# Routing from the raw residual rows, gathers without padded rows, and a later wait for the stored rows, in a one-core diffusion layer

## The chip, the cores and the metric

The kernel runs on one core of a Trainium2 chip. The metric is the device time of one execution in microseconds (us). Before the change it is 688.88 us, the median of three runs (688.39 to 688.99).

## The reference

All arrays are fp32. One layer works on 512 latent tokens and 256 context tokens of width 1024. The first half (modulated RMS norm, input projection, neighbourhood attention beside a gated linear recurrence, output projection) gives the residual rows x. What the change touches comes after it:

```python
hx = _rms(x, norm_ffn[l]) * (1 + sc_fx) + sh_fx
x = x + g_fx * _moe(hx, router_w, router_b, exp_w1[l], exp_w3[l], exp_w2[l])

def _moe(h, router_w, router_b, w1, w3, w2):
    aff = jax.nn.sigmoid(h @ router_w)            # 512 x 16
    sel = aff + router_b
    # best of 4 groups by the sum of its two best, then the two best experts in it
    wts = ...                                     # their affinities, normalised
    for e in range(16):
        y = (jax.nn.silu(h @ w1[e]) * (h @ w3[e])) @ w2[e]
        out = out + gates[..., e:e + 1] * y
```

`sc_fx` and `sh_fx` are pieces of `silu(c) @ w_mod + b_mod`. An expert has 6 MB of weights, all sixteen 96 MB, which are read once.

## The kernel before

It is written engine by engine: each has its own program, and semaphores tie them. The order of the work is the order in which those programs are written; there is no scheduler.

**Modulation sums.** DVE multiplies pieces of `w_mod` by the condition vector and adds them up over rows into `acct`; PE (`reduce_mod`, L1398 to L1407, called four times between the projections) sums over partitions by eight matmuls against a column of ones, and DVE (`reduced`, L893) adds the bias. The result is `ab2`: per column a scale (index 0) and a shift (index 1), as [128, 8]. DVE completes it at L996 and L997.

**Attention and out projection.** PE runs 17 rounds: scores, transposed probabilities, values, and a share of the out projection (`project_out`, L1540) in each. Two of the 64 out projection products are left for after the rounds. DVE turns the out projection into residual rows `x2` (`residual`, L1036), four tiles j of 128 tokens in two halves each.

**Router.** ACT squares and roots the rows (`square2`, `root2`), DVE takes the reciprocal and makes `xn = x2 * 1/rms` (`normalise`, L1048). PE transposes `xn` in eight blocks (`router`, L1573), ACT and DVE each evacuate four blocks, one by one, and apply scale and shift on the way (`router_rows`, L706 and L1052). PE multiplies by the router weights `rw` (`logits`, L1587), ACT takes the sigmoid (L723). DVE then selects experts in some 60 small operations, PE counts and sorts (L1616 to L1625), and DVE writes `slot_tok`: for each tile of 32 slots the row numbers of its tokens (L1234). A slot without a token points to one of 512 spare rows behind the real ones.

**Rows through DRAM.** Each row is stored as four quarters of 256. POOL stores `xn` into `xn_quarters`, and one tile again into the spare rows (L472), then `x2` into `out_quarters` (L476, L478). It then waits for all these stores and for the slots, and gathers the first four tiles (L486), 128 quarter rows each. Later gathers follow one per tile, and each tile's result is added to `out_quarters` by an accumulating scatter (L490).

**Experts.** For each tile DVE transposes the gathered rows and applies scale and shift (L1251, L1253, L1260). PE multiplies by w1 and w3 (`products`, L1640), then by w2 (`rows_out`, L1655). Every expert has at least two tiles.

**Weights.** SP fetches 48 chunks of 2 MB (`fetch`, L309), three per expert: two halves of w1 and w3, then w2. There are 11 places for them. Chunks 0 to 10 wait for whatever lies in their place before; the others wait for PE to be done with the chunk 11 before them:

```python
sp.wait_ge(y_ps, 2 * NT)
for n in range(5, 8):
    fetch(n)
sp.wait_ge(xn_out, 8 * NT + 16)
sp.wait_ge(xn_out1, 8 * NT)
sp.wait_ge(h2_ps, 2 * NT)
fetch(8)
sp.wait_ge(acc_in, 16 * NT + 16)
fetch(9)
sp.wait_ge(slots_turned, 1)
fetch(10)
```

## Time and profile before

| | |
|---|---|
| median of three runs | 688.88 us (688.39 to 688.99) |
| the profiled execution's own time | 685.32 us |
| its span, first to last instruction | 683.6 us |
| busy in the span | PE 605.4 us, PE weight loads 362.8, DVE 385.0, ACT 199.0, POOL 180.0 |
| moved by DMA | 168.08 MB, mean 246 GB/s |
| mean granted clock of TensorE | 0.949 of 2.4 GHz |
| attention rounds | about 264 to 371 us |
| router and selection, first gather landed | 371 to 417 us |
| experts | 419 to 670 us, last stores to the end |

PE is TensorE's matmul side. Busy time of matmuls is modelled, and neighbouring groups overlap a little, so a group's end is best read from the start of the next. A span's times are counted from its first instruction; the execution's own time is 1.72 us longer than its span.

### The profile page before, as it was taken

To read this page: it belongs to the slowest core of one execution; us is meant where nothing else is said; L and a number is where in the kernel's file an instruction comes from. 1 tells how busy PE (TensorE), PEld (TensorE's weight loads), DVE (VectorE), ACT (ScalarE), POOL (GpSimd) and SP (SyncE) were. 2 spreads that over 40 slices of the span, in tenths; PEclk is the share of its full clock that TensorE was granted. 3 is DMA by queue.
4 is the path that set the end of the run, shared out by engine and by line. 5 is a ranking of instruction groups with operands and counts; after the bars stand their busy time and mean duration, and the time that the engine had idled before them with its cause. 6 is when DMAs were issued, how large, how long until landed. Compare 5 with 4: busy or idle time off the path is not lost.

```text
span 683.6 us, 14771 instructions
## 1 busy us (share of the span) xinstructions
PE 605.4 (89%) x5803; PEld 362.8 (53%) x5803; DVE 385.0 (56%) x909; ACT 199.0 (29%) x499; POOL 180.0 (26%) x202
## 2 busy tenths in 40 slices
PE   0799999999999998999999824999999999879981
PEld 0455544455554444555556822667767776635650
DVE  4714995686869874786775472444444444414430
ACT  5312201158796203555465400001000110000000
POOL 4044782000000001000000203454445554424421
PEclk9999999999999999999999557999999999989996
DMA  8989338530305175900007986699999999999974
GB/s 300 387 277 310 124 123 291 201 124 0 123 1 185 53 255 160 253 4 1 1 0 296 424 339 279 240 389 390 390 393 390 387 389 390 387 409 391 394 247 138
DMA packets 52979, 168.08 MB, mean 246 GB/s; under 512 B 4212, under 2 KB 26384, under 8 KB 42688
## 3 DMA queue, kind: packets, MB, share of 16 engines
q1 hardware_dynamic: 41136, 145.78, 55.6%
q0 software_dynamic: 11664, 21.53, 12.2%
q8 instruction: 37, 0.61, 0.3%
q14 instruction: 14, 0.11, 0.0%
q10 hardware_dynamic: 128, 0.04, 0.0%
HBM read 155.53 MB, written 13.12 MB: 247 GB/s over the span
## 4 chain that ended last, share of the span: by engine, by line
PE 69%; DVE 10%; DMA 8%; ACT 4%; issue 4%; SPq 3%; ACTq 0%; POOLq 0%; DVEq 0%
PE bank L1640 18%; PE bank L1446 12%; PE bank L1655 9%; PE bank L1556 7%; DMA ring<-in_exp_w_dram 6%; PE bank L1371 6%; PE bank L1378 4%; SPq L313 3%; PE bank L1533 2%; PE bank L1508 2%; PE bank L1519 2%; DVE acct L868 1%; PE bank L1404 1%; DMA pre<-xn_quarters,slot_tok 1%; ACT hx L553 1%
## 5 line engine op out<-in xcount | busy, mean ns | idle before, releaser
L1446 PE MATMUL bank<-ring,hx 128*128 128x512 f32 x256 | 117.8, 617 | 2.5 <-DVE mix L923 1.9
L1640 PE MATMUL bank<-pre 128*32 128x256 f32 x1248 | 77.1, 392 | 17.7 <-DVE pre L1260 9.6
L1446 PEld LDWEIGHTS bank<-ring,hx 128*128 128x128 f32 x256 | 49.7, 197 | 62.7 <-issue 60.3
L729 ACT ACTIVATE pre<-bank 128x128 f32<-128x128 f32 x44 | 12.2, 277 | 223.8 <-PE bank L1640 198.2
L1260 DVE TENSOR_TENSOR pre<-pre,ab 128x256 f32<-128x256 f32 x44 | 19.2, 437 | 94.6 <-PE bank L1640 83.7
L1640 PE MATMUL bank<-ring,pre 128*32 128x256 f32 x1152 | 68.1, 380 | 3.0 <-issue 1.7
L1640 PEld LDWEIGHTS bank<-pre 128*32 128x32 f32 x1248 | 46.6, 113 | 42.7 <-DVE pre L1260 11.2
L1556 PE MATMUL bank<-ring,mix 128*128 128x512 f32 x128 | 60.7, 594 | 0.0
L1640 PEld LDWEIGHTS bank<-ring,pre 128*32 128x32 f32 x1152 | 43.6, 110 | 23.5 <-issue 4.8
L490 POOL DMA_INDIRECT out_quarters<-pre,cur_s x22 | 35.4, 1610 | 71.2 <-DVE pre L1278 52.8
L490 POOL DMA_INDIRECT out_quarters<-hx,cur_s x22 | 35.7, 1624 | 51.5 <-DVE hx L1278 49.2
L1655 PE MATMUL bank<-pre 128*32 128x256 f32 x704 | 42.6, 379 | 0.9 <-DVE pre L1271 0.9
L1271 DVE STREAM_TRANSPOSE pre<-pre 128x128 f32<-128x128 f32 x44 | 18.2, 415 | 44.6 <-PE bank L1655 44.6
L1371 PE MATMUL bank<-hx,ring 128*128 128x256 f32 (+1 forms) x128 | 42.0, 488 | 1.4 <-DVE hx L846 1.4
L460 POOL DMA_DIRECT2D pre<-pre x1 | 0.6, 561 | 157.0 <-ACT pre L665 157.0
L486 POOL DMA_INDIRECT hx<-xn_quarters,cur_g x30 | 31.1, 1035 | 14.2 <-issue 8.8
L1371 PEld LDWEIGHTS bank<-hx,ring 128*128 128x128 f32 x128 | 24.1, 190 | 19.1 <-issue 16.7
L1655 PE MATMUL bank<-ring,pre 128*32 128x256 f32 x544 | 34.1, 390 | 0.0
L1655 PEld LDWEIGHTS bank<-pre 128*32 128x32 f32 x704 | 27.1, 110 | 12.0 <-DVE pre L1271 1.4
L470 POOL DMA_DIRECT2D xn_quarters<-pre x4 | 2.2, 544 | 110.6 <-DVE pre L1049 110.6
L868 DVE SCALAR_TENSOR_TENSOR acct<-ring,cs,acct 128x256 f32<-128x256 f32 x56 | 29.4, 525 | 2.0
L1556 PEld LDWEIGHTS bank<-ring,mix 128*128 128x128 f32 x128 | 21.7, 190 | 14.7 <-issue 14.7
(282 smaller groups left out, 1013.2 us busy)
## 6 DMA issues: line engine op xcount, KB each, us to landing
pre<-in_exp_w_dram SPq DMA_DIRECT2D x28, 1024.0 KB
ring<-in_exp_w_dram SPq DMA_DIRECT2D x24, 1024.0 KB
ring<-in_w_mod_dram SPq DMA_DIRECT2D x16, 1024.0 KB, 5.1
pre<-in_exp_w_dram SPq DMA_DIRECT2D x8, 2048.0 KB
ring<-in_exp_w_dram SPq DMA_DIRECT2D x6, 2048.0 KB
ring<-in_w_in_dram SPq DMA_DIRECT2D x5, 2048.0 KB, 14.1
ring<-in_w_mod_dram SPq DMA_DIRECT2D x4, 2048.0 KB, 18.1
mix<-in_exp_w_dram SPq DMA_DIRECT2D x6, 1024.0 KB
```

Source lines behind the costliest of these rows:

```text
L313: sp.dma_start(chunk13(e, part)[:, :, w, :], src[0, ORDER[e]].rearrange("(p k) n -> p k n", p=P)[:, 4 * part:4 * part + 4, :]).then_inc(cs ...
L486: g.indirect_dma_start(out=xg[par], out_offset=None, in_=xn_dram, in_offset=bass.IndirectOffsetOnAxis(ap=index.bitcast(U32), axis=0)).then ...
L490: g.indirect_dma_start(out=acc_dram, out_offset=bass.IndirectOffsetOnAxis(ap=cur_s[par][:].bitcast(U32), axis=0), in_=ysb[par], in_offset= ...
L868: ins = v.scalar_tensor_tensor(out=dst, in0=src[:, k, :], scalar=cs[:, k, 0:1], in1=dst, op0=ALU.mult, op1=ALU.add)
L1260: v.tensor_tensor(blocks(hsT), blocks(xm), wide(1), ALU.add).then_inc(hs_ready, 1)
L1271: v.transpose(eT.rearrange("p (b t) -> p b t", b=4), eact.rearrange("p (t b) -> p b t", b=4)).then_inc(t2_ev, 1)
L1371: ins = te.matmul(B[bank][:, 0:n], slot[:, k, P * m:P * (m + 1)], hxT[:, k, lo:lo + n], start=(k == 0), stop=(k == KD - 1))
L1378: ins = te.matmul(B[4 + m % 2][:, :], slot[:, k, P * m:P * (m + 1)], hxT[:, k, 0:T], start=(k == 0), stop=(k == KD - 1))
L1446: ins = te.matmul(B[bank][:, :], hxT[:, k, P * j:P * (j + 1)], slot[:, k, :], start=(k == 0), stop=(k == KD - 1))
L1556: ins = te.matmul(B[YB[hf]][:, :], mix[:, k, P * j:P * (j + 1)], out_at[hf][0][:, k, :], start=(k == MW), stop=(k == MW - 1))
L1640: ins = te.matmul(H_[R * q:R * (q + 1), 0:2 * P].rearrange("p (w n) -> p w n", w=2), hsT[:, R * k:R * (k + 1)], w[:, k % 4, :, P * q:P * ( ...
L1655: ins = te.matmul(Y_[R * q:R * (q + 1), 0:QD], eT[:, R * c:R * (c + 1)], w[:, c, QD * q:QD * (q + 1)], start=(c == 0), stop=(c == 3))
```

## The change

The shared parts of it:

- The router transposes `x2` instead of `xn`, half a tile (four blocks) at a time, so that a token's 1/rms is applied to its 16 logits instead of its 1024 values (`logit_rows`). The scale goes into the weights (`rws = rw * scale`), the shift into one row of 16 numbers (`shift_sum`, summed over partitions by one more matmul, L1624 of the new kernel). Evacuation is a plain copy of 512 columns. The logits come from PSUM banks 5 and 6.
- The sets of transposes for tile 0 stand inside the last rounds, those for tile 1 ahead of the last two out projection products.
- ACT normalises tiles 2 and 3, behind the sigmoid; DVE keeps 0 and 1.
- Columns are spread over partitions in two halves of 4 x 128 instead of 8 x 128. So the modulation sums take four matmuls per call, `xn` is stored with its columns reordered, and a half of w1 or w3 is one contiguous megabyte.
- The gathers get a bound: a row number beyond the real rows is left out. The spare rows of `xn_quarters` and the store into them go.
- SP issues chunk 8 ahead of its wait for the transposes. POOL waits for the stored `x2` after the first four gathers.

```diff
-    xn_dram = nc.dram_tensor("xn_quarters", (TRASH + 4 * P, QD), F32, kind="Internal").ap()
+    xn_dram = nc.dram_tensor("xn_quarters", (TRASH, QD), F32, kind="Internal").ap()
@@ SP
-                                     src[0, ORDER[e]].rearrange("(p k) n -> p k n", p=P)[
-                                         :, 4 * part:4 * part + 4, :]).then_inc(csem[n % NH], 16)
+                                     src[0, ORDER[e], 512 * part:512 * (part + 1), :].rearrange(
+                                         "(p k) n -> p k n", p=P)).then_inc(csem[n % NH], 16)
-            sp.wait_ge(xn_out, 8 * NT + 16)
+            sp.wait_ge(xn_out, 8 * NT)
             sp.wait_ge(xn_out1, 8 * NT)
+            fetch(8)
             sp.wait_ge(h2_ps, 2 * NT)
-            fetch(8)
@@ POOL
-            g.dma_start(xn_dram[TRASH:TRASH + 4 * P, :].rearrange("(p q) n -> p (q n)", q=CB), xn[:, 0, :]).then_inc(
-                xn_out, 16)
...
-                    ap=index.bitcast(U32), axis=0)).then_inc(xg_in[par], 16)
+                    ap=index.bitcast(U32), axis=0), bounds_check=TRASH - 1, oob_is_err=False).then_inc(xg_in[par], 16)
...
-            pool.wait_ge(acc_in, 16 * NT + 16)
             pool.wait_ge(slots_turned, 1)
             for n in range(4):
                 gather(slot_tok[:, n:n + 1], n)
             pool.wait_ge(plan_in, 1)
+            pool.wait_ge(acc_in, 16 * NT + 16)
@@ ACT
-                for k in range(MW):
-                    a.activation(h2T[:, j % 2, k, :], B[RB[j % 2]][:, P * k:P * (k + 1)],
-                                 ACT.Identity, scale=ab2[:, 0, k:k + 1], bias=ab2[:, 1, k:k + 1]).then_inc(h2_ev, 1)
+                a.activation(h2T[:, j % 2, 4 * h:4 * h + 4, :].rearrange("p k t -> p (k t)"), B[XB[j][h]][:, :],
+                             ACT.Copy).then_inc(done, 1)
...
-            act.wait_ge(lg_ps, NT)
-            a.activation(rt[:, 0:NT * NE], B[0][:, 0:NT * NE], ACT.Sigmoid).then_inc(aff_ready, 1)
+            act.wait_ge(logit_in, NT + 1)
+            a.activation(rt[:, 0:NT * NE], rt[:, 256:256 + NT * NE], ACT.Sigmoid).then_inc(aff_ready, 1)
+            for j in (2, 3):
+                act.wait_ge(roots_set, j)
+                a.activation(xn[:, j, :].rearrange("p (q h m) -> p h q m", q=CB, h=2),
+                             x2[:, j, :].rearrange("p (h q m) -> p h q m", q=CB, h=2), ACT.Copy,
+                             scale=small[:, 24 + j:25 + j]).then_inc(xn2_ready, 1)
@@ DVE
+            link(v.tensor_tensor(rws, rw[:], ab2[:, 1, :].unsqueeze(2).to_broadcast([P, KD, NE]), ALU.mult))
+            link(v.tensor_reduce(shift_sum, rws.rearrange("p k e -> p e k"), AX.X, ALU.add))
+            v.tensor_tensor(rws, rw[:], ab2[:, 0, :].unsqueeze(2).to_broadcast([P, KD, NE]), ALU.mult).then_inc(
+                rws_ready, 1)
...
+            def logit_rows(j):
+                v.scalar_tensor_tensor(out=rt[:, 256 + NE * j:256 + NE * (j + 1)], in0=B[LB[j]][:, NE * j:NE * (j + 1)],
+                                       scalar=small[:, 24 + j:25 + j], in1=a1[:].rearrange("p k s -> p (k s)"),
+                                       op0=ALU.mult, op1=ALU.add).then_inc(logit_in, 1)
@@ PE
-                for k in range(KD):
-                    ins = te.matmul(B[7][HD * (n % 2):HD * (n % 2 + 1), k:k + 1],
-                                    acct[:, :].rearrange("p (m k) -> p m k", k=KD)[:, :, k], ones[:, 0:1], start=True,
-                                    stop=True)
+                for k in range(4):
+                    ins = te.matmul(B[7][:, k:k + 1], acct[:, :].rearrange("p (m k) -> p m k", k=4)[:, :, k], ones[:, 0:1],
+                                    start=True, stop=True)
...
+            def router(j, h):
+                if j == 1 and h == 0:
+                    pe.wait_ge(prob_done, NA)
+                if j >= 2:
+                    pe.wait_ge(h2_ev if h == 0 else h2_ev2, j - 1)
+                pe.wait_ge(x2_ready, 2 * j + h + 1)
+                for k in range(4):
+                    ins = te.transpose(B[XB[j][h]][:, P * k:P * (k + 1)],
+                                       x2[:, j, :].rearrange("p (h m k) -> p h m k", h=2, k=4)[:, h, :, k], ident[:])
+                ins.then_inc(h2_ps, 1)
```

PE's program at the end of the attention rounds, before. L1519 transposes probabilities, L1533 multiplies by the values, L1556 is the out projection, L1582 the router's transposes, L1593 the logits:

```order
L1533 MATMUL bank<-pre 64x128
L1582 MATMUL bank<-ident,pre 128x128 [waits xn2_ready]
L1582 MATMUL bank<-ident,pre 128x128 x7
L1556 MATMUL bank<-ring,mix 128x512 [waits ot_ev]
L1556 MATMUL bank<-ring,mix 128x512
L1582 MATMUL bank<-ident,pre 128x128 [waits xn2_ready,ot_ev,pt_ev]
L1582 MATMUL bank<-ident,pre 128x128 x7
L1593 MATMUL bank<-rw,pre 128x16 [waits h2_ev,rw_in]
```

The same place in the new kernel, where L1581 is the out projection, L1593 the transposes and L1616 the logits:

```order
L1558 MATMUL bank<-pre 64x128
L1593 MATMUL bank<-ident,hx 128x128 [waits x2_ready,prob_done]
L1593 MATMUL bank<-ident,hx 128x128 x3
L1593 MATMUL bank<-ident,hx 128x128 [waits x2_ready]
L1593 MATMUL bank<-ident,hx 128x128 x3
L1581 MATMUL bank<-ring,mix 128x512 [waits ot_ev]
L1581 MATMUL bank<-ring,mix 128x512
L1624 MATMUL bank<-pre,ones 128x16
L1616 MATMUL bank<-pre 128x16 [waits h2_ev] x4
```

Tile 0's transposes have moved up, to before the last transposed probabilities, and tile 1's stand where tile 0's stood; they wait for residual rows and not for normalised ones. The matmul of the shift comes in.

DVE's program from the last residual rows to the first operation of the selection, before (L1044 and L1045 residual, L1064 reciprocal, L1049 normalise, L1058 evacuation, L1110 to L1116 constants, L1128 selection):

```order
L1045 TENSOR_TENSOR hx<-hx,pre 128x512 [waits dch]
L1064 RECIPROCAL small<-small 128x1 [waits rt2]
L1049 TENSOR_SCALAR pre<-hx,small 128x1024 [waits dch]
L1058 TENSOR_SCALAR pre<-bank,ab 128x128 [waits h2_ps]
...
L1058 TENSOR_SCALAR pre<-bank,ab 128x128 [waits lg_ps,h2_ps]
L1058 TENSOR_SCALAR pre<-bank,ab 128x128 x3
L1110 MEMSET pre 128x4 x16
L1113 MEMSET pre 128x4 [waits dch]
L1113 MEMSET pre 128x4 x3
L1116 MEMSET counts 128x16 [waits dch]
L1128 TENSOR_TENSOR pre<-pre,rb 128x64 [waits rw_in,aff_ready,dch]
```

And in the new kernel (L1063 residual, L1076 evacuation, L1080 reciprocal, L1085 scaled logits, L1137 to L1143 constants, L1154 selection):

```order
L1063 TENSOR_TENSOR hx<-hx,pre 128x512 [waits dch]
L1076 COPY pre<-bank 128x512 [waits lg_ps,h2_ps]
L1080 RECIPROCAL small<-small 128x1 [waits rt2]
...
L1080 RECIPROCAL small<-small 128x1 [waits rt2]
L1085 SCALAR_TENSOR_TENSOR pre<-bank,small,a 128x16 [waits lg_ps,roots_set]
L1137 MEMSET pre 128x4 x16
L1140 MEMSET pre 128x4 [waits dch]
L1140 MEMSET pre 128x4 x3
L1143 MEMSET counts 128x16 [waits dch]
L1154 TENSOR_TENSOR pre<-pre,rb 128x64 [waits aff_ready,dch]
```

The normalise operations are gone from this stretch, and the constants stand behind an operation that waits for the last logits (`lg_ps`), where before they stood behind an evacuation.

## Rows read from the trace of the kernel before

**Rows 1.** Its DMA view, 434 to 657 us, by queue: packets, MB, share of 16 engines

```profile
q1 hardware_dynamic: 8699, 76.45, 83.2%
q0 software_dynamic: 7550, 10.29, 20.3%
```

**Rows 2.** Timeline of PE: start, us, what, count, [idle before and its releaser]

```profile
604.13 3.64 PE L1640 MATMUL bank<-pre 128*32 128x256 f32 x32 [4.05 <-DMA pre<-in_exp_w_dram]
...
657.01 1.93 PE L1640 MATMUL bank<-ring,pre 128*32 128x256 f32 x32 [1.37 <-DMA ring<-in_exp_w_dram]
```

**Rows 3.** Timelines of PE and, last row, DVE, 373 to 391 us

```profile
373.99 1.05 PE L1582 MATMUL bank<-ident,pre 128*128 128x128 f32 x8
374.87 1.86 PE L1593 MATMUL bank<-rw,pre 128*128 128x16 f32 x16
377.62 1.68 PE L1582 MATMUL bank<-ident,pre 128*128 128x128 f32 x8 [0.90 <-DVE pre L1049]
379.10 3.44 PE L1593 MATMUL bank<-rw,pre 128*128 128x16 f32 x16
382.37 1.95 PE L1582 MATMUL bank<-ident,pre 128*128 128x128 f32 x8
384.11 6.85 PE L1593 MATMUL bank<-rw,pre 128*128 128x16 f32 x32
...
372.47 1.37 DVE L1058 TENSOR_SCALAR pre<-bank,ab 128x128 f32<-128x128 f32 x4 [0.78 <-PE bank L1582]
```

**Rows 4.** Windows: PE, PEld, DVE, ACT, POOL busy, granted clock, DMA share, GB/s

```profile
376.00:378.00 2.00, 1.10 (x10) 1.04 (x10) 1.97 (x5) 1.45 (x4) 0.23 (x1) 1.00 1.09 463
378.00:380.00 2.00, 2.00 (x12) 2.00 (x11) 1.96 (x7) 1.63 (x5) 0.40 (x2) 0.50 0.94 401
658.00:660.00 2.00, 2.00 (x44) 1.20 (x40) 0.62 (x2) 0.37 (x2) 0.00 (x0) 1.00 0.74 239
```

**Rows 5.** Timeline of DVE, constants and start of the selection

```profile
385.67 0.29 DVE L1110 MEMSET pre<- 128x4 f32 x16
...
391.31 0.23 DVE L1128 TENSOR_TENSOR pre<-pre,rb 128x64 f32<-128x64 f32 x1 [5.04 <-issue]
```

**Rows 6.** Chain of waits (start, us, what), and SP's timeline, fetch 9

```profile
410.86 6.29 DMA pre<-xn_quarters,slot_tok
...
408.10 0.80 SPq L313 DMA_DIRECT2D hx<-in_exp_w_dram  x2
```

**Rows 7.** Chain of waits, 240 to 262 us

```profile
245.97 2.01 PE bank L1404 x16
```

**Rows 8.** Timelines of ACT and DVE, third gate after the third modulation sum

```profile
175.50 0.69 ACT L616 ACTIVATE pre<-bank,half_b 128x512 f32<-128x512 f32 x1
...
174.18 1.28 DVE L953 TENSOR_TENSOR_SCAN pre<-pre 128x512 f32<-128x512 f32 x1
```

**Rows 9.** Timeline of DVE, the first score

```profile
265.55 0.42 DVE L1010 TENSOR_TENSOR hx<-bank,pre 128x256 f32<-128x256 f32 x1 [7.57 <-PE bank L1508]
```

**Rows 10.** Tile xn_quarters, stores issued by POOL

```profile
DMA to landing us min/median/max: 9.0/10.6/13.7
```

**Rows 11.** DMA view, 424 to 433 us: busy tenths in 40 bins, and POOL's queue

```profile
DMA  0000000000096500000300000000000000000000
...
q0 software_dynamic: 48, 0.13, 5.3%
```

**Rows 12.** The page's groups: the shift of a tile, once per tile

```profile
L1260 DVE TENSOR_TENSOR pre<-pre,ab 128x256 f32<-128x256 f32 x44 | 19.2, 437 | 94.6 <-PE bank L1640 83.7
```

**Rows 13.** DMA view, 664 to 674 us: POOL's queue, scatters alone

```profile
q0 software_dynamic: 432, 0.39, 34.9%
```

**Rows 14.** Timeline of POOL, one scatter and one gather in the stream

```profile
582.06 1.58 POOL L490 DMA_INDIRECT out_quarters<-pre,cur_s  x1 [2.76 <-DVE pre L1278]
583.95 1.10 POOL L486 DMA_INDIRECT hx<-xn_quarters,cur_g  x1 [0.30 <-issue]
```

More of the change, by code:

```diff
@@ L194, in build @@
          cur_g_ready, cur_s_ready, acc_in, gf_ps, gf_ev, lane_set, sil_warm, pad_ready, bank_z,
[L195 removed]
+         row_sum_ready, scale_ready, hc_ready, h2_ev2, rows_taken, xm_scaled, act_ready, ffn_in,
+         half_ps, rws_ready, logit_in, roots_set) = [sem(n) for n in names]
         xg_in = [sem(f"rows_in{par}") for par in range(4)]
@@ L1048, in normalise @@
             def normalise(j):
-                v.tensor_scalar(xn[:, j, :], x2[:, j, :], small[:, 24 + j:25 + j], None,
+                v.tensor_scalar(xn[:, j, :].rearrange("p (q h m) -> p h q m", q=CB, h=2),
+                                x2[:, j, :].rearrange("p (h q m) -> p h q m", q=CB, h=2), small[:, 24 + j:25 + j], None,
                                 ALU.mult).then_inc(xn2_ready, 1)
@@ L1082, in _ @@
             router_rows(0)
+            router_rows(1)
             residual(2 * NT - 2)
             residual(2 * NT - 1)
+            router_rows(3)
             roots_in(2, 2, 3)
-            normalise(2)
-            router_rows(1)
+            dve.wait_ge(lg_ps, NT - 1)
+            v.tensor_copy(a1[:].rearrange("p k s -> p (k s)"), B[5][:, NT * NE:(NT + 1) * NE]).then_inc(logit_in, 1)
+            dve.wait_ge(logit_in, 1)
+            for j in range(NT - 1):
+                logit_rows(j)
             roots_in(3, 3, 4)
-            normalise(3)
-            router_rows(2)
-            router_rows(3)
+            dve.wait_ge(lg_ps, NT)
+            logit_rows(NT - 1)
             NTE = NT * NE
```

87 lines of the change are left out of this document (42 added, 45 removed).

## Prediction

> **What bounds the kernel now.** The page shows PE busy nearly everywhere, so I read it stage by stage. Four stages matter here.
>
> The expert stage, from 434 us on, is bound by the transfer of the expert weights. In 434 to 657 the two data queues together fill the 16 DMA engines (83.2% and 20.3%) [rows 1]. PE consumes weights faster than they come: it stood 4.05 us waiting for them before 604.13, and 1.37 us before its last weight chunk at 657.01 [rows 2]. So the end follows the time at which this stream starts, and the traffic it shares the DMA engines with. The stream starts when PE has finished its third tile (about 432 us): until then every buffer is full.
>
> Before it lies a serial stretch, 371 to 419 us: out projection, transposes (L1582), logits (L1593), sigmoid, selection on DVE, one matrix that sorts tokens into slots, and the first gather. PE sets the pace up to the sigmoid: 16 logit matmul records took 1.74 to 1.86 us at 374.87 and 3.3 to 3.4 us from 379.10 on [rows 3], because the granted clock was 1.00 (2.4 GHz) until 378 us and 0.50 (1.2 GHz) after it [rows 4]. DVE starts its selection 0.35 us after the last logit matmul, its constants having been written at 385.67 [rows 5]. The first gather then took 6.29 us to land, on the chain [rows 6].
>
> Further ahead, the modulation sums (L1404) take 2.01 us of PE each, and the fourth stands on the chain at 245.97 [rows 7]. After its end PE goes straight on with projections to 262.3 us.
>
> **The change, part by part.**
>
> *Modulation sums.* Each of four calls now issues 4 matmuls instead of 8, over 128 columns of weights instead of 64. Before, 16 records took 2.01 us, 0.126 us each; 128-column weight loads with a tiny moving side cost about the same (1.86 us for 16 at full clock [rows 3, 7]). So each call saves 1.0 us. Only the fourth counts: after the third, ACT waited for PE but its next step (L616 at 175.50) also waited for the DVE scan that began at 174.18 and took 1.28 us [rows 8], so that stage is paced by ACT and DVE, not PE; bounds for the first three are 0 and 0.1. The three added DVE operations (L1012 to L1014 of the new kernel, under 1.2 us together) come when DVE is idle for 7.6 us before the first score [rows 9], and would cost 1.2 us without that idle time. Everything behind 246 us moves **1.0 us** earlier (bounds 0 and 1.1).
>
> *Transposes and logits.* The transposes read x2, so none waits for a normalise; the 0.90 us that PE stood before the third set [rows 3] goes. In exchange the first two sets (1.05 us each) stand ahead of the last two out projection products, where one stood before, so the last residual rows are ready about 0.6 us later (1.05 us, less what DVE gains by copying 512 columns once instead of four pieces in 1.37 us [rows 3]). They are not late: the last half set of transposes needs them some 8 us further on. Added on PE: one matmul for the shift, 0.23 us. On PE's own times I get, from 371.1 us: values end 372.1, second set 373.2, out projection 374.9, shift 375.1, logits(0) 376.9, third set 377.9. If the clock falls at 378 us as it did, three logit groups at 3.3 to 3.4 and two half sets at 0.87 (3.27 + 1.74 + 6.78 = 11.8 us) end at 389.8, against 390.96: 1.15 us saved. Then comes what is new behind the last logit matmul: DVE scales the last rows (0.2 us, as its small operations take, and 0.1 us of handover) and writes its constants only after that, 0.6 us that formerly were hidden [rows 5]. So selection starts 0.95 us after PE instead of 0.35. Net **0.6 us** saved. Bounds: 0.6 us lost, if the 1.15 doesn't come; 6.3 us gained, if the clock stays at 1.00 through the logits (12.96 us from 378 on at half clock become about 6.1 from 377.9).
>
> *Residual and normalised rows.* Rows 2 and 3 are normalised by ACT behind the sigmoid, about 390.3 to 392.7 us (512 columns took it 0.69 us [rows 8], so some 1.2 us each), so their stores are issued at 392 to 393 instead of 377.8 to 379.9; those behind them on POOL's queue, five stores of x2, go too, at 393 to 396. The stores took 9.0 to 13.7 us to land on a full DMA [rows 10]; 393 + 13.7 = 407 is still before the slots are ready at 409. So nothing waits for them. One store of 0.5 MB is gone, and there is a hole of 2 us in the DMA's work. On SP, the ninth weight chunk (fetch 8) waits for these stores and comes at 395 to 397 instead of 394.19; fetch 9 waits for all x2 stores and I put it at 405.5 to 408 against 408.10 [rows 6]; fetch 10 follows the slots. They are first used by the third and fourth experts, tens of us later, so their own lateness is free. POOL's wait for the x2 stores is behind the first gathers; before it had ended (408.1) ahead of the slots (410.0), so moving it gives 0 now.
>
> *The first gather.* It waited behind weights: 6.29 us loaded; alone on the DMA, one issued at 424.91 moved its data in bins 11 to 14 of 40 over 424 to 433, that is by 427.2, 2.3 us after issue [rows 11]. With fetch 9 ahead by 0 to 2.6 us, less of it is in the queue. Bounds: 0 and 4.0 us saved; I take **0.8**, nearer 0, because fetch 10 is still issued just ahead of it, and tile 0 has no padded row. The Trainium skill, "DMA: Bandwidth & Descriptors", Queues, rings and completion order, says that each engine alternates between its queues packet by packet; by that the gather's few packets would never sit behind a backlog and this term would be 0. The 6.29 against 2.3 us speaks against it.
>
> *The gathers in the stream.* 44 tiles of 128 quarter rows [rows 12] make 5632, of which 4096 are real (512 tokens, 2 experts, 4 quarters), so 27% of the gathered rows fall away. One gather alone took 5.3% of 9 us on all 16 engines, 0.48 us [rows 11]; a scatter, 34.9% of 10 us for 0.39 MB, three of them, 1.16 us [rows 13]. In the stream the pair cost 20.3% of 223 us over 39.5, 1.15 us [rows 1], of which the gather's share is 0.34 us (0.48/1.64). Saved: 39 x 0.27 x 0.34 = 3.6 us at most if spread evenly (5.1 at 0.48), 0 if a left out row costs what a moved one does. But a weight chunk has landed only when its slowest part has, and the parts end unevenly: the DMA share falls to 0.74 at 658 to 660 and takes some 5 us to run out [rows 4]. The padded rows are always the last of a tile's 32. From the routing of the reference (expert counts 122, 102, 129, 57, 67, 90, 87, 88, 19, 17, 17, 17, 51, 67, 59, 35) rows 0 to 3 are empty in 12.5% of the 44 tiles and rows 28 to 31 in 45%. If the part that gates serves the first rows, 39 x 0.125 x 0.34 = 1.7 us is saved. I take **2.5 us**, about midway between 1.7 and 3.6.
>
> The weight transfers for w1 and w3 read whole megabytes instead of every second 8 KB; pieces keep 8 KB, and the engines are full with both, so 0 (bounds: 2 us either way). xn's changed column order alters patterns, not counts.
>
> **Sum:** 1.0 + 0.6 + 0.8 + 2.5 = 4.9 us. The profiled execution took 685.32 us (span 683.6), so 680.4; the median of the runs is 3.56 us above it, at 688.88, so I forecast 684.0.
>
> **The rivals.**
>
> *A, the stream saves what its slowest part saves, or nothing.* For: the uneven ends. 1.0 + 0.6 + 0 to 0.8 + 0 to 1.7 gives 684.8 to 687.3; I take 686.3. The Trainium skill, "DMA: Bandwidth & Descriptors", The descriptor swizzle, ties each DMA engine to fixed partitions, four neighbours at a time; by that the engines of rows 0 to 3 would save only the 1.7 us. No row here shows single engines.
>
> *B, the clock stays up longer in the logits.* PE has no pause of 0.90 us and its dense out projection ends 0.9 us later. One later step is worth about 1.7 us, all of it 5.7. 682.3, down to 678.3. Against: the mix of work is the same, and from 382 to 391 it never brought the clock back.
>
> *C, PE waits longer at the end and drops its clock.* Near 600 us, after a wait of 4.05, 32 records took 3.64 us instead of 1.93 [rows 2], and lost 1.7 us beside the wait. If the earlier wait shrinks, PE is ready for its last chunk some 3 us sooner and waits there; 13 us of tiles follow, of which a part at half clock costs 2 to 3.5 us: 686.8.
>
> *D, slower: the check makes POOL's gathers slow.* POOL spends per tile 1.10 us on the gather, 1.58 on the scatter and 0.30 before each [rows 14], 3.3 of the 5.4 us per tile (418.8 to 657.0, 44 tiles). Up to 2.0 us more per gather is hidden but for the first, which is on the path. At 3.3 us per gather it would cost 2.2 us there and 0.2 x 40 = 8 later: 694. From an added 2.2 us it outweighs the gains. Nothing in the trace speaks for it; an index compared with a constant is little work.
>
> *E, the rows are not left out, or the front gains nothing*: about 688.
>
> **How the numbers follow.** Forecast mechanism 0.42, A 0.20, B 0.17, C 0.10, D 0.05, E 0.06. What a measurement can tell from no change is about 0.2%, 1.4 us: 687.5 to 690.3 is "same". Faster: all of the forecast and B (0.59), most of A (0.15) and over half of C (0.06): 0.80. Same: the rest of A, C and E, 0.13. Slower: D and a little of the unknown weight order, 0.07. The range takes in A, C and B's first step: 680.5 to 688.0.
>
> **What would show it.** Four modulation calls of 8 records in 1.0 us. L1616 groups without a pause before the third transposes; last logit matmul about 2 us earlier than 390.96 (1.0 from the sums, 1.15 here), with the constants written after it. Gather landing in 5 to 6 us. In the stream, the gathers' queue with fewer bytes (about 8.9 MB instead of 10.3) and the last weight wait at about 652. The forecast is wrong if the queue's bytes don't fall, if the weight queue's rate changes, or if the granted clock around 380 us or after 650 us is another.

## The result, and the profile after

The changed kernel takes 683.09 us (median of four executions, 682.84 to 684.1) beside 688.93 us for the kernel before (688.39 to 689.43): a ratio of 0.9918, 95% interval 0.9901 to 0.9935. The forecast was 684.0. The profiled execution took 682.84 us, its span 681.0, so the two profiled executions differ by only 2.5 us where the medians differ by 5.8: the one of before was 3.6 under its median, the one of after is a typical one. That is why the table below has each kernel twice, the second time from a later session (their spans: 686.4 and 678.0). All numbers are differences of start times in the timelines, in us; "the logits' end" is the start of the matmuls that stand behind them on PE (L1637, L1610 before).

| stretch | before | again | after | again |
|---|---|---|---|---|
| start to first score on DVE | 265.55 | 266.42 | 263.26 | 264.94 |
| to the logits' end | 125.34 | 125.31 | 122.52 | 121.75 |
| to the selection's start | 0.42 | 0.42 | 1.08 | 1.08 |
| to the slots written | 18.41 | 18.46 | 18.72 | 18.73 |
| to the gather's issue | 1.14 | 1.14 | 1.22 | 1.21 |
| gather, issue to landing | 6.29 | 6.33 | 7.02 | 4.60 |
| to the stream's first fetch | 15.06 | 15.05 | 14.82 | 15.18 |
| to PE's last wait for weights, its end | 224.80 | 225.32 | 223.11 | 222.90 |
| to the end of the span | 26.59 | 27.95 | 29.25 | 27.61 |

So against the second profile of before, the more typical one, the change gains 1.5 to 3.2 us before the first score, 2.8 to 3.6 in the router (0.66 of it paid back for the constants), and 2.2 to 2.4 in the stream. The gather varies by itself, and 0.3 us is lost between the selection's start and the slots. The end is longer in one profile of before and in both of after.

The gain before the first score is mostly not the change's own. In fourteen profiles, with those of the experiments below, the granted clock fell to half in one to three short stretches between 28 us and the first score. They add up to 10.2, 10.2 and 13.6 us in the three profiles whose program is still that of before up to this point (first score at 265.6, 266.4 and 268.6), and to 3.4 us in six, 6.8 in two and 10.2 in three of the eleven of the changed one. In these last three the first score came at 266.2 to 267.0, no earlier than in before with the same 10.2 us. Whether the change itself makes these stretches fewer is not shown.

The fourth modulation sum on the chain of waits of the changed kernel ([rows 7] before: 16 records, 2.01 us):

```profile
245.86 1.64 PE bank L1430 x8
```

A record with 128 columns of weights costs 0.205 us on average, one with 64 columns 0.126: half as many records do not take half the time.

PE through the router ([rows 3] before), start, us, what, count:

```profile
370.00 1.23 PE L1593 MATMUL bank<-ident,hx 128*128 128x128 f32 x8
371.07 1.88 PE L1581 MATMUL bank<-ring,mix 128*128 128x512 f32 x4
372.79 0.29 PE L1624 MATMUL bank<-pre,ones 128*128 128x16 f32 x2
372.93 1.94 PE L1616 MATMUL bank<-pre 128*128 128x16 f32 x16
374.71 1.19 PE L1593 MATMUL bank<-ident,hx 128*128 128x128 f32 x8
375.74 1.86 PE L1616 MATMUL bank<-pre 128*128 128x16 f32 x16
377.44 1.02 PE L1593 MATMUL bank<-ident,hx 128*128 128x128 f32 x4
378.26 3.43 PE L1616 MATMUL bank<-pre 128*128 128x16 f32 x16
381.53 1.09 PE L1593 MATMUL bank<-ident,hx 128*128 128x128 f32 x4
382.42 3.43 PE L1616 MATMUL bank<-pre 128*128 128x16 f32 x16
385.78 1.08 PE L1637 MATMUL bank<-gfx,ones 128*32 128x256 f32 x8
```

No group has an idle time in front of it, and the third transposes start behind the first logits at once. The clock, [rows 4] before:

```profile
376.00:378.00 2.00, 2.00 (x18) 2.00 (x18) 0.00 (x0) 0.59 (x2) 0.00 (x0) 0.90 1.02 401
378.00:380.00 2.00, 2.00 (x12) 2.00 (x11) 0.00 (x0) 1.50 (x3) 0.00 (x0) 0.50 0.98 414
```

It fell at about the same time, but the program is some 2 us further on, so two logit groups, not one, ran in 1.9 us. The same time on the axis is a coincidence of these two profiles: counted from the start of the last out projection products, the clock fell after 5.7, 5.8 and 7.0 us in the three profiles of before's program and after 6.5 to 10.9 us in the eleven of the changed one. DVE then writes its constants behind the last scaled row ([rows 5] before: 5.6 us ahead of the selection). DVE's timeline, from the second profile of the changed kernel (a_again):

```profile
387.06 0.37 DVE L1137 MEMSET pre<- 128x4 f32 x16
387.50 0.10 DVE L1140 MEMSET pre<- 128x4 f32 x4
387.66 0.07 DVE L1143 MEMSET counts<- 128x16 f32 x1
387.77 0.23 DVE L1154 TENSOR_TENSOR pre<-pre,rb 128x64 f32<-128x64 f32 x1
```

The selection starts behind the last of them. The gather of the first profile on the chain, and SP's fetches 9 and 10 beside it ([rows 6] before):

```profile
406.80 7.02 DMA pre<-xn_quarters,slot_tok
```

```profile
406.69 0.80 SPq L317 DMA_DIRECT2D hx<-in_exp_w_dram  x2
407.55 1.24 SPq L317 DMA_DIRECT2D pre<-in_exp_w_dram  x2
```

The stream, 434 to 650 us ([rows 1] before), and PE's waits in it ([rows 2] before):

```profile
q1 hardware_dynamic: 8604, 74.95, 84.2%
q0 software_dynamic: 7648, 8.88, 19.6%
```

```profile
597.24 1.93 PE L1667 MATMUL bank<-pre 128*32 128x256 f32 x32 [2.30 <-DMA pre<-in_exp_w_dram]
...
645.93 1.93 PE L1667 MATMUL bank<-ring,pre 128*32 128x256 f32 x32 [2.51 <-DMA ring<-in_exp_w_dram]
651.75 3.64 PE L1667 MATMUL bank<-ring,pre 128*32 128x256 f32 x32 [3.89 <-DMA ring<-in_exp_w_dram]
```

The wait of 4 us that stood near 604 has become one of 3.89 before the last chunk, and what follows it runs at half clock at first: 32 records in 3.64 us instead of 1.93.

### The profile page after: what moved, and what is told of

It reads as the page before. It is cut to its first block, busy times and chain, and to the rows that moved or that the text cites. A ratio compares the mean times of both kernels' runs of the same rounds, so it can differ in the third digit from the quotient of the medians.

```text
span 681.0 us, 14746 instructions
## 1 busy us (share of the span) xinstructions
PE 598.6 (88%) x5773; PEld 358.3 (53%) x5773; DVE 382.8 (56%) x902; ACT 197.9 (29%) x490; POOL 185.5 (27%) x201
## 4 chain that ended last, share of the span: by engine, by line
PE 63%; DMA 13%; DVE 11%; ACT 5%; issue 4%; SPq 1%; ACTq 0%; POOLq 0%; DVEq 0%
PE bank L1667 16%; PE bank L1471 9%; PE bank L1682 8%; PE bank L1581 7%; DMA ring<-in_exp_w_dram 6%; PE bank L1397 6%; DMA pre<-in_exp_w_dram 5%; PE bank L1404 4%; PE bank L1558 2%; PE bank L1533 2%; PE bank L1544 2%; DVE acct L882 1%; PE bank L1616 1%; DMA pre<-xn_quarters,slot_tok 1%; SPq L317 1%
## 5 line engine op out<-in xcount | busy, mean ns | idle before, releaser
L1471 PE MATMUL bank<-ring,hx 128*128 128x512 f32 x256 | 114.4, 602 | 5.6 <-DVE mix L936 4.9
L1667 PEld LDWEIGHTS bank<-pre 128*32 128x32 f32 x1248 | 46.1, 111 | 39.7 <-DVE pre L1286 12.2
L1581 PE MATMUL bank<-ring,mix 128*128 128x512 f32 x128 | 60.7, 594 | 0.0
L490 POOL DMA_INDIRECT hx<-xn_quarters,cur_g x30 | 34.4, 1148 | 14.2 <-issue 8.9
L476 POOL DMA_DIRECT2D xn_quarters<-pre x4 | 2.2, 542 | 121.8 <-DVE pre L1067 97.2
L1682 PEld LDWEIGHTS bank<-pre 128*32 128x32 f32 x704 | 27.0, 113 | 13.6 <-issue 1.6
L1397 PEld LDWEIGHTS bank<-hx,ring 128*128 128x128 f32 x128 | 24.1, 190 | 19.1 <-issue 16.7
L1581 PEld LDWEIGHTS bank<-ring,mix 128*128 128x128 f32 x128 | 21.7, 190 | 14.7 <-issue 14.7
## 6 DMA issues: line engine op xcount, KB each, us to landing
pre<-in_exp_w_dram SPq DMA_DIRECT2D x8, 2048.0 KB, 26.6
```

What stands on the lines that cost most here:

```text
L490: g.indirect_dma_start(out=xg[par], out_offset=None, in_=xn_dram, in_offset=bass.IndirectOffsetOnAxis(ap=index.bitcast(U32), axis=0), boun ...
L1397: ins = te.matmul(B[bank][:, 0:n], slot[:, k, P * m:P * (m + 1)], hxT[:, k, lo:lo + n], start=(k == 0), stop=(k == KD - 1))
L1471: ins = te.matmul(B[bank][:, :], hxT[:, k, P * j:P * (j + 1)], slot[:, k, :], start=(k == 0), stop=(k == KD - 1))
L1581: ins = te.matmul(B[YB[hf]][:, :], mix[:, k, P * j:P * (j + 1)], out_at[hf][0][:, k, :], start=(k == MW), stop=(k == MW - 1))
L1667: ins = te.matmul(H_[R * q:R * (q + 1), 0:2 * P].rearrange("p (w n) -> p w n", w=2), hsT[:, R * k:R * (k + 1)], w[:, k % 4, :, P * q:P * ( ...
L1682: ins = te.matmul(Y_[R * q:R * (q + 1), 0:QD], eT[:, R * c:R * (c + 1)], w[:, c, QD * q:QD * (q + 1)], start=(c == 0), stop=(c == 3))
```

## The experiments

Ratios are to the kernel before in the same session (medians of three later sessions: 689.24, 687.48 and 688.78). Executions of one kernel spread over up to 9 us there, so differences under 1% between medians are weak, and I read each experiment first from its trace. One table for all; "logits": from the first score to their end; "chunk 9": its issue less that of the gather; "stream": first fetch to the end of PE's last wait for weights; "wait": how long that was; "rest": from there to the end of the span. In a_warm the gather's landing is hidden behind other work on the chain.

| kernel | median, us | ratio (95%) | logits | chunk 9 | gather | stream | wait | rest |
|---|---|---|---|---|---|---|---|---|
| before, first profile | 688.93 | 1 | 125.3 | -2.8 | 6.29 | 224.8 | 1.37 | 26.6 |
| b_again | 689.77 | 1.000 (0.997 to 1.003) | 125.3 | -2.9 | 6.33 | 225.3 | 3.86 | 28.0 |
| b_bound | 686.44 | 0.9979 (0.9951 to 1.0007) | 124.2 | -1.5 | 6.35 | 222.6 | 4.01 | 28.3 |
| after, first profile | 683.09 | 0.9918 (0.9901 to 0.9935) | 122.5 | -0.1 | 7.02 | 223.1 | 3.89 | 29.3 |
| a_again | 680.16 | 0.9889 (0.9858 to 0.992) | 121.8 | +0.9 | 4.60 | 222.9 | 3.80 | 27.6 |
| a_again2 | 680.52 | 0.9866 (0.9825 to 0.9906) | 122.5 | +0.1 | 6.75 | 222.7 | 3.80 | 28.0 |
| a_nobound | 679.27 | 0.9868 (0.9831 to 0.9906) | 119.8 | +4.1 | 4.36 | 225.6 | 1.40 | 26.0 |
| a_nobound2 | 681.15 | 0.9901 (0.9865 to 0.9937) | 122.6 | +2.0 | 2.85 | 225.0 | 1.51 | 26.0 |
| a_w13 | 678.38 | 0.9845 (0.9809 to 0.9881) | 121.6 | +1.4 | 2.87 | 222.7 | 3.40 | 27.8 |
| a_oldwait | 682.68 | 0.9923 (0.9886 to 0.996) | 119.6 | -1.0 | 6.47 | 222.9 | 3.81 | 27.5 |
| a_late | 679.33 | 0.9871 (0.9836 to 0.9907) | 119.2 | +3.1 | 3.01 | 222.8 | 3.91 | 28.6 |
| a_consts | 679.56 | 0.9867 (0.983 to 0.9905) | 119.1 | +3.6 | 3.84 | 222.9 | 3.90 | 27.8 |
| a_warm | 676.2 | 0.9846 (0.9801 to 0.9892) | 122.4 | +2.0 | hidden | 222.3 | 3.65 | 28.6 |
| a_all | 674.52 | 0.9802 (0.9765 to 0.9838) | 122.6 | +2.9 | 2.82 | 222.6 | 3.75 | 27.7 |

### The bound alone, and the kernel before again

b_again is the kernel before, unchanged:

> The kernel before, unchanged, for a second profile. The profiled pair differs by 2.5 us (685.32 to 682.84), the medians by 5.8. Theory L (luck of the clock): the granted clock fell to half for 3.4 us at three places before 266 us in the profile of before and once in that of after, so such steps come and go between executions; then this profile has a time between 685 and 689 us with these steps at other places, and the first record of the experts stands at 418 to 421 us. Theory F (the profile of before was an odd one): its time is within 0.5 us of 688.9, and what it shows in the expert stage (last weight wait, tail) is 3 us longer than 657 and 684 us.

b_bound adds only the bound:

```diff
-                    ap=index.bitcast(U32), axis=0)).then_inc(xg_in[par], 16)
+                    ap=index.bitcast(U32), axis=0), bounds_check=TRASH - 1, oob_is_err=False).then_inc(xg_in[par], 16)
```

> The kernel before with nothing changed but the bound on the gathers (the spare rows are still stored, and not read). Theory S (slowest part): the weight stream gains 1.5 to 2.5 us, so 686.5 to 687.4 against 688.9, ratio 0.9965 to 0.998; the POOL queue moves 8.9 MB instead of 10.3 in the stream. Theory E (spread evenly): 3.6 us less, ratio 0.995. Theory N (a left out row costs as much as a moved one): ratio 1.000.

b_again: 689.77, ratio 1.000. Neither theory holds whole: the time, 688.17, is in the range of L, but the three half-clock stretches stand where they stood in before (at 140, 164 and 249 us). Its trace shows that the first profile of before was a favourable one: b_again loses 1.4 us more behind the last weight wait. b_bound: 686.44, ratio 0.9979, at the place of theory S, but the interval still holds 1. Its stream is 2.7 us shorter than that of b_again.

### The changed kernel without the bound, twice

The bound undone, one tile stored again into the spare rows, and the waits for the stored rows counting it (the two waits are left out here):

```diff
-                    ap=index.bitcast(U32), axis=0), bounds_check=TRASH - 1, oob_is_err=False).then_inc(xg_in[par], 16)
+                    ap=index.bitcast(U32), axis=0)).then_inc(xg_in[par], 16)
...
+            g.dma_start(xn_dram[TRASH:TRASH + 4 * P, :].rearrange("(p q) n -> p (q n)", q=CB), xn[:, 0, :]).then_inc(
+                xn_out, 16)
```

> The changed kernel with the bound taken back: spare rows stored again, all rows gathered. Theory S: 1.5 to 2.5 us slower than the changed kernel (684.6 to 685.6), ratio to before 0.9935 to 0.995. Theory E: 686.7. Theory N: 683.1, ratio 0.9915. The first gather should take about as long as with the bound (7.0 us), since tile 0 has no padded row.

> The changed kernel without the bound on the gathers and with the spare rows stored again, for the second time, now beside the changed kernel itself. Theory S (left-out rows relieve the stream by the 1.7 us of its slowest part): slower than the changed kernel beside it by 1 to 2.5 us. Rival N (the bytes saved are not on the path, or the small packets that stand in for left-out rows and the slower GpSimd work give the gain back): within 1 us. Rival H (the bound costs): faster by over 1 us. The first time the ratio was 0.9868, without the changed kernel beside it; 0.9889 was seen for the changed kernel in another session, so N or H is likelier than S.

With the second one ran the changed kernel itself:

> The changed kernel again, as the standard for the three kernels that share the chip with it. Its executions differ by where half-clock stretches fall; median within 679.5 to 683.5, ratio to the kernel before 0.987 to 0.992.

By the medians nothing can be told: 681.15 against 680.52 in one session. By the traces it is clear. In the four profiles without the bound the stream took 224.8 to 225.6 us (mean 225.2), in the ten with it 222.3 to 223.1 (mean 222.8): the bound saves 2.4 us there. Most of it is given back behind the last wait. Timeline of PE of a_nobound2:

```profile
597.03 3.64 PE L1669 MATMUL bank<-pre 128*32 128x256 f32 x32 [4.81 <-DMA pre<-in_exp_w_dram]
...
649.72 1.93 PE L1669 MATMUL bank<-ring,pre 128*32 128x256 f32 x32 [1.51 <-DMA ring<-in_exp_w_dram]
```

Its clock from there on, and that of the changed kernel (window, length, PE, PEld, DVE, ACT, POOL busy, granted clock, DMA share, GB/s):

```profile
650.00:656.00 6.00, 6.00 (x116) 3.61 (x112) 1.41 (x4) 0.37 (x2) 0.96 (x1) 1.00 0.50 158
656.00:658.00 2.00, 2.00 (x44) 1.22 (x40) 0.29 (x1) 0.46 (x3) 0.59 (x1) 1.00 0.45 37
```

```profile
650.00:656.00 6.00, 4.25 (x40) 1.92 (x44) 0.53 (x2) 0.37 (x2) 0.00 (x0) 0.56 0.59 214
656.00:658.00 2.00, 2.00 (x28) 1.00 (x24) 0.09 (x1) 0.00 (x0) 0.00 (x0) 0.62 0.01 1
```

Where the last wait was 1.4 to 1.5 us the clock stayed at 1.00 (2.4 GHz) and the rest took 26.0 to 26.6 us; where it was 3.4 to 4.0 the clock fell to half, for 3.4 us (6.8 in the first profile of the changed kernel), and the rest took 27.5 to 29.3 (mean of the ten with the bound 28.1). So of the 2.4 us some 1.9 are lost again, and 0.5 is left, less than these medians can tell. b_again shows that the loss goes with the wait and not with the bound: without the bound, but with a wait of 3.86 us, its rest was 28.0. It shows too that the kernel before can have this loss; beside such an execution the bound keeps its 2.4 us. How often before has it is not known, from two profiles, one with and one without.

POOL's queue in a_nobound2's stream moved 10.17 MB, 1.3 MB more than with the bound, in fewer packets:

```profile
DMA packets 15957, 84.62 MB, mean 392 GB/s; under 512 B 2185, under 2 KB 7137, under 8 KB 8381
...
q0 software_dynamic: 7434, 10.17, 20.6%
```

The changed kernel has 2570 packets under 512 bytes in as long a stretch (434 to 650 us), 385 more, and 20.6 to 19.6% of busy share: some small packets come along with the left-out rows, not nothing. The gathers in the stream issue in 1.16 us on POOL instead of 1.07, and between slots and the first gather's issue stand 1.21 us instead of 1.14: all that the check costs on the path is 0.07 us.

### The old order of w1 and w3

```diff
-                                     src[0, ORDER[e], 512 * part:512 * (part + 1), :].rearrange(
-                                         "(p k) n -> p k n", p=P)).then_inc(csem[n % NH], 16)
+                                     src[0, ORDER[e]].rearrange("(p k) n -> p k n", p=P)[
+                                         :, 4 * part:4 * part + 4, :]).then_inc(csem[n % NH], 16)
```

In it the products pair columns of the rows with other rows of w1 and w3 than the reference does.

> The changed kernel, but the halves of w1 and w3 are read as before (every second 8 KB of the matrix). The products then pair columns with the wrong weight rows; the work is the same. Theory 0: no change, 683.1 within 0.7 us. Rival W: whole megabytes are read faster, and 1 us or more of the gain is theirs: 684.1 or above, with the last weight wait later than 651.75 us.

Its stream took 222.7 us, like the others with the bound. The order of the weight rows is worth nothing either way. Its median, 678.38, is no further from a_nobound's of the same session (679.27) than their spreads allow; rival W is out.

### The first gather, chunk 9 and the wait for the stores

a_again is the changed kernel, as the standard of its session:

> The changed kernel itself, in the company of its variants. The two variants run so far stood at 679.3 (rows all gathered) and 678.4 us (old weight order) against 689.2 before, where the changed kernel had 683.1 against 688.9. Theory G (gather and weights collide): the changed kernel sends both late weight chunks at the moment of its first gather, which took 7.02 us; in the variants it took 4.36 and 2.87 us. Then this one is 681 to 684 us, ratio 0.989 to 0.992. Theory P (the place or the day makes the difference, not the variants): it is 678 to 680 us like them, ratio 0.985 to 0.987.

Its median, 680.16, stands just above the range of theory P and below that of G, and its gather took 4.60 us: one kernel's gather can differ by 2.4 us between two profiles.

a_late lets SP fetch chunks 9 and 10 behind the landing of the first gather:

```diff
+            sp.wait_ge(slots_turned, 1)
+            sp.wait_ge(xg_in[0], 16)
             fetch(9)
-            sp.wait_ge(slots_turned, 1)
             fetch(10)
```

> The changed kernel, but SP issues weight chunks 9 and 10 only when the first gather has landed. Theory G: the gather takes 2.3 to 2.9 us instead of 7.0, so the experts begin 4 us earlier, and the end follows by 3 to 4 us against the changed kernel run beside it; the two chunks are first used after 440 us and their 4 MB are moved by then. Rival Q (the engines are busy with other things anyway, or the end is set by a stream that starts later for other reasons): less than 1 us.

a_oldwait puts POOL's wait for the stored x2 back in front of the gathers:

```diff
+            pool.wait_ge(acc_in, 16 * NT + 16)
             pool.wait_ge(slots_turned, 1)
             for n in range(4):
                 gather(slot_tok[:, n:n + 1], n)
             pool.wait_ge(plan_in, 1)
-            pool.wait_ge(acc_in, 16 * NT + 16)
```

> The changed kernel, with the wait for the stored residual rows back in front of the first gathers. In the profile the stores had landed at 406.7 us and the slots were ready at 405.8. Theory M: the gather starts 0.8 to 1.5 us later, and lands behind both weight chunks; 1 to 2 us slower than the changed kernel beside it. Rival 0 (as the prediction had it): no difference, within 0.5 us.

a_late: 679.33 against 680.16, which says nothing. Its gather landed after 3.01 us, near what theory G said, and from the selection's start to the stream's first fetch it took 38.4 us against 39.7 in a_again; the 3 to 4 us at the end did not come. The column "chunk 9" of the table orders all gathers. With chunk 9 issued before the gather or within 0.1 us behind it, six took 6.3 to 7.0 us. With chunk 9 0.9 us later one took 4.60; 1.4 us or more later, six took 2.8 to 4.4, and the two longest of these were issued while x2 stores had 3.6 and 4.1 us to go (chunk 9 marks their landing). So the time goes with the place in the queue: whole weight chunks put ahead delay the gather by some 3 to 4 us, and a_late and a_all, which move the chunks on purpose, are both among the short ones.

By the Trainium skill, "DMA: Bandwidth & Descriptors", Queues, rings and completion order, each engine alternates between its queues packet by packet. The prediction took this to mean that no backlog of weights could delay the gather, and held 6.29 against 2.3 us against it. But by the same section of the Trainium skill such a packet is a whole run of descriptors, typically 9 to 17. A weight piece is 8 KB and the 16 engines moved 392 GB/s together, so one engine needs about 3.0 us for nine pieces (an estimate, the nine from that page of the Trainium skill). A single such run ahead of the gather would delay it by about what was seen. So the rows agree with this rule as well as with a strict order of issue, and no run separates the two.

a_oldwait: 682.68 against 680.16 (679.18 to 686.46 against 679.69 to 680.72; the intervals of the ratios overlap). Its chain of waits shows the price at once:

```profile
390.25 17.73 DMA out_quarters<-hx
...
408.99 6.47 DMA pre<-xn_quarters,slot_tok
```

The slots were written at 404.35, the third earliest of all, and yet the gather was issued at 408.99, 4.64 us later instead of 1.21, because the last x2 store landed only at 407.98. In the first profile of the changed kernel, in a_again and in a_consts these stores are issued between 389.1 and 392.4 us and the slowest lands after 15.2, 16.1 and 18.5 us, at 406.7, 408.6 and 409.7. With the old wait a gather comes 0.95 us behind that landing; so the moved wait is worth 0.8 us in the first profile of the changed kernel, 1.8 in a_again and 4.5 in a_consts (estimates from their issue times). Besides, it lets the gather go ahead of chunk 9, which waits for the same stores.

### Constants early

```diff
+            for e in range(NE):
+                ins = v.memset(rt[:, 384:448].rearrange("p (j e) -> p j e", j=NT)[:, :, e:e + 1], float(NE - e))
+            link(ins)
```

(and the two others with it, put before DVE's wait for the last row's logits).

> The changed kernel with VectorE's selection constants written while it waits for the logits instead of after the last row of them. Theory K (they stand on the path): the selection starts about 0.4 us after the last logit matmul instead of 1.0, and everything behind it comes 0.6 us earlier: median 0.6 us under the changed kernel beside it, seen in the trace though hardly in the medians. Rival: the selection waits for ACT's or DVE's evictions anyway, 0.

```profile
385.08 0.25 DVE L1118 MEMSET pre<- 128x4 f32 x16
385.41 0.10 DVE L1121 MEMSET pre<- 128x4 f32 x4
385.57 0.07 DVE L1123 MEMSET counts<- 128x16 f32 x1
385.68 0.24 DVE L1085 SCALAR_TENSOR_TENSOR pre<-bank,small,a 128x16 f32<-128x16 f32 x1
386.24 0.22 DVE L1153 TENSOR_TENSOR pre<-pre,rb 128x64 f32<-128x64 f32 x1 [0.32 <-ACT pre L730]
```

The selection starts 0.87 us after the logits' end instead of 1.08: now it waits for ACT's sigmoid. In a_all it was 0.73. So theory K gets 0.2 to 0.35 us of its 0.6; the rest of the cost was never the constants'. Ratio 0.9867 against 0.9866 beside it: the same.

### PE kept busy through its waits, and all three together

a_warm gives PE idle matmuls of 512 columns (four behind the logits, four behind the counts, nine behind the slots) whose results nobody reads:

```diff
+            def keep_busy(n):
+                for _ in range(n):
+                    te.matmul(B[3][:, :], ones[:], gax[:, 0:512], start=True, stop=True)
```

> The changed kernel with 17 dummy matmuls of 512 columns into an unused bank while PE has nothing to do: 4 ahead of the counting matmuls, 4 ahead of the sorting ones, 9 behind them. They are additional work, and read only constants. Theory K (the clock at half costs in this stretch): the sorting matmuls take about 1.9 us instead of 3.4, the first tile 3.5 instead of 5.4, and the experts begin 2 us earlier, with the first tiles done 4 us earlier; 3 to 4 us faster at the end, if the weights' stream starts so much earlier. Rival Q: the end doesn't follow, since DMA sets it; under 1 us.

a_all has them (4, 4 and 6), the early constants and the late chunks:

> Three things together on the changed kernel: constants early (0.6 us), weight chunks 9 and 10 issued behind the landing of the first gather (gather in 3 us instead of 4.6 to 7), and 14 idle 512-column matmuls that keep the TensorE clock up over the serial stretch (alone 4 us). If they add up: 674 to 676, ratio about 0.981. If the clock is what decides and the gather lands fast anyway: no more than the warm kernel alone, 0.9846.

Timeline of PE of a_all, L1643 being the idle work:

```profile
386.74 5.84 PE L1643 MATMUL bank<-gax,ones 128*128 128x512 f32 x8
394.08 0.43 PE L1648 MATMUL bank<-pre,tri 128*128 128x64 f32 x2 [1.50 <-DVE pre L1185]
...
400.68 2.87 PE L1658 MATMUL bank<-pre 128*32 128x120 f32 x64 [2.23 <-DVE pre L1231]
403.48 6.02 PE L1643 MATMUL bank<-gax,ones 128*128 128x512 f32 x12
409.78 1.93 PE L1674 MATMUL bank<-pre 128*32 128x256 f32 x32 [0.28 <-DVE pre L1286]
411.53 1.91 PE L1674 MATMUL bank<-ring,pre 128*32 128x256 f32 x32
```

The clock came back to 1.00 at 391.1 us in a_all and 391.4 in a_warm, while in the twelve profiles without idle work it stood at half until 401.8 or later. The first tile, at half clock in these twelve (3.45 to 3.64 us for 32 records), runs at full: 1.93. The sorting matmuls took 2.87 us instead of 3.43, not the 1.9 expected. a_warm: 676.2 against 680.16 for a_again, five of six executions below all of a_again's; in its profile nine idle matmuls last until 412.36, some 2 us longer than a gather of 2.9 us would have needed (an estimate: issued at 405.74, and 1.63 us from landing to the tile). a_all, with six there: **674.52 (673.25 to 677.68), ratio 0.9802 (0.9765 to 0.9838)** against 0.9866 for the changed kernel beside it (0.9825 to 0.9906); the intervals overlap a little, but five of its six executions lie below all six of that one. The mean clock of its profiled execution is 0.974 against 0.959. It is the fastest version here, 14.3 us under the kernel before in its session.

## Why the prediction was right

The total was right, 684.0 against 683.09, and so was the direction. Its terms were not all, and one of its own signs of being wrong came true: the granted clock after 650 us was another (0.56 instead of 1.00 in the first profile of the changed kernel). The last logit matmul ended 5.1 us earlier, not 2, and the gather took 7.02 us, not 5 to 6.

- **Sums, 1.0 us.** Mis-sized. From ACT's last gate (244.29 and 249.01 in before and b_bound, 244.19 after) to the first score passed 19.57 us in b_bound and 19.1 in every profile of the changed kernel: 0.5 us. (Before itself and b_again have 21.26, with 3.4 us of half clock in it; b_bound and the eleven have none there.) The step that failed is "128-column weight loads with a tiny moving side cost about the same": it took the price from records with as many columns of weights in another place, 0.116 us; here they cost 0.205. The two places also differ in the moving columns (16 there, 1 here) and in how the weights lie in memory, and which of these makes the price stays open.
- **Router, 1.15 us on PE, less 0.6 for the constants.** PE's sequence came as worked out, with every group within 0.1 us when shifted by the 2.1 us by which it began earlier. But the clock fell one logit group later in the program, which is 1.6 us more: rival B's first step. In the table the logits end 2.7 to 6.2 us sooner after the first score than in before and b_again, and the four of 119.1 to 119.8 us are those where the clock held through three of the four groups or more. So B's chance of 0.17 was too low: its first step came every time, and nearly all of its 5.7 us (6.2 less the 1.15) in four of eleven profiles. Why the clock held longer in these four stays open; before's program has such luck too, 124.2 us in b_bound. The constants cost what was said, 1.08 instead of 0.42 us, but a_consts shows that only 0.2 to 0.35 of it is theirs. No experiment takes the new router alone: its gain is read from the traces.
- **The moved wait, 0 us.** Wrong. The step compared the landing of the old stores (408.1) with the old slots (410.0). In the new kernel the slots are ready some 4 us sooner, and the x2 stores landed at 406.7 to 409.7. Without the moved wait they would have become the bound of the front: 0.8 to 4.5 us. The "393 + 13.7 = 407" behind it is also misread: 13.7 us is the slowest store of xn_quarters [rows 10], and by the text itself the x2 stores are issued at 393 to 396. Those of before, issued at 380.9 to 383.0, took 16.8 to 25.0 us to land (view of tile out_quarters, 375 to 415 us). In the new kernel they were issued at up to 391.5 us and the slowest took 15.2 us (first profile), so 407 came out nearly right by luck.
- **The first gather, 0.8 us.** Not borne out as a fixed term: 0.73 us longer in the first profile of the changed kernel, 0.4 longer and 1.7 shorter in its two others, and 1.9 to 3.4 shorter in a_nobound, a_nobound2 and a_w13, which leave the order of SP's fetches and the gather as it is. What goes with it is whether it is issued ahead of chunk 9, which the text saw ("with fetch 9 ahead by 0 to 2.6 us") but priced as a matter of how far ahead, not before or behind. Fetch 10, which it saw just ahead of the gather, was issued 0.75 us behind it.
- **The stream, 2.5 us.** Right: 2.4 us, with the bytes as said (8.88 MB; 8.9 forecast). It lies above the 1.7 us of rival A, which the first pair of profiles alone, with 1.7, would have seemed to confirm. But 2.5 was chosen as a midpoint, and no run shows which part of the DMA engines gates the stream, so the size was met without its reason being shown.
- **Rival C** got a chance of 0.10 and happened in all ten profiles with the bound, at 1.9 us on average (2 to 3.5 were forecast). That is the main error of the sum, counted from the first profile of before: the step that failed is to treat it as a rival, when it is a sequel of the stream's gain. The text said so itself: PE is ready for its last chunk some 3 us sooner. Against executions like b_again, which lose the clock there already, it costs nothing.
- **D** fell: the check costs POOL 0.1 us per gather, hidden, and 0.07 on the path. **The order of w1 and w3**: 0, as said.

So the sum, with what was measured, is 0.5 for the modulation sums, 2.1 in the router with the constants paid, -0.7 to 1.7 in the gather, and 2.4 in the stream, less 1.9 at the end and 0.4 between the selection's start and the gather's issue (most of it in the sorting matmuls, 3.43 us instead of 3.18): 2.0 to 4.4. Three things can add to it. Up to 3.4 us come when the clock holds through the logits. Up to 1.9 come against an execution of before that loses the clock at its end too, as b_again did. Up to 1.7 come when the gather is as fast as in a_nobound2. The 5.8 us of the first session and the 7.3 and 8.3 of the others lie within that, but the ranges are wide, and the short half-clock stretches before the first score add to them. How often each of these happens stays open: there is one profile for each kernel and session. That the forecast came within 1 us is luck in part: it is owed to errors of both signs.

## What to carry to other kernels

A gain in a stream moves the wait: ask where PE will stand next, and whether the granted clock is lost in what follows (here 1.9 of 2.4 us). When work on the path becomes faster, reprice every wait beside it (here the stores of x2), since "it ended earlier before" is no longer an argument. And take one profiled execution as one sample: with spreads of 4 to 9 us, a stage's length between two marks in its trace (222.8 against 225.2 in fourteen profiles) tells what medians can't.

## What the runs showed of the hardware

- A first gather of 128 rows of 1 KB took 6.3 to 7.0 us when 2 MB of weights were issued ahead of it or within 0.1 us behind it, and 2.8 to 4.6 us when they were issued 0.9 us or more behind it (13 profiles).
- Rows left out by the bound are not quite free: 385 more packets under 512 bytes for 1.3 MB less, and POOL's queue fell from 20.6% to 19.6%. One per cent of 225 us is 2.2 to 2.3, near the 2.4 us of the stream; left-out rows that cost nothing would have saved 3.6 by the prediction's working.
- fp32 matmuls with one moving column, at full clock: 0.126 us a record with 64 columns of weights, 0.205 with 128.
- Idle matmuls while PE waited brought the clock back to 1.00 at 391.1 to 391.4 us, instead of 401.8 or later, and the first tile took 1.93 us instead of 3.45 to 3.64.
- Before the last weight chunk, a wait of 1.4 to 1.5 us left the clock alone and one of 3.4 to 4.0 us was followed by half clock, in all fourteen profiles. Earlier in the stream, waits of 4.0 to 5.5 us were followed by 3.20 to 3.64 us for 32 records. Waits of 0.2 to 2.6 us mostly left the clock alone (1.93 us), but not in a_w13, a_warm and b_bound: 3.50, 3.51 and 3.60 us behind waits of 2.17, 2.27 and 2.34. So the length of the wait alone does not decide.
